# Product-key experts: the weight grid moves from TensorE one-hot matmuls to GpSimd scatter-add DMAs in DRAM

## The reference, cut to what matters

```python
s = einsum('thpc,hpnc->thpn', q, keys)         # 8 heads, 2 halves, 128 keys each
sv, si = top_k(s, 16)
cand = sv[:, :, 0, :, None] + sv[:, :, 1, None, :]
cv, ci = top_k(cand.reshape(T, 8, 256), 16)    # 16 experts a head and token
eid = e1 * 128 + e2
g = softmax(cv)
coef = g * gelu(x . u_tab[eid])
y = sum over heads and k of coef * v_tab[eid]  # residual added after
```

## Time and profile before

| | us |
|---|---|
| median of 3 runs | 3870.16 |
| lowest and highest | 3866.17, 3870.42 |
| profiled execution | 3867.6 |
| its span in the profile | 3865.9 |
| PE busy in the span | 3839.1 (99%) |
| DVE, ACT, POOL busy | 2532.3, 2065.4, 170.8 |
| granted clock of TensorE, mean | 0.997 |

### The profile page before, as it was taken

How to read it: one execution, slowest core, us unless ns; L and a number is a source line. 1 busy time by engine, 2 the same in 40 slices (tenths; PEclk the granted TensorE clock), 3 DMA queues, 4 the chain that set the end, 5 groups by cost and what they waited for, 6 DMA issues and landing times.

```text
span 3865.9 us, 58649 instructions
## 1 busy us (share of the span) xinstructions
PE 3839.1 (99%) x19628; PEld 3270.9 (85%) x19628; DVE 2532.3 (66%) x3843; ACT 2065.4 (53%) x3240; POOL 170.8 (4%) x150
## 2 busy tenths in 40 slices
PE   8999999999999999999999999999999999999999
PEld 8989988888888888888899889888888888888887
DVE  4565789878885555555564555889788875555555
ACT  5354444478885444444454544444688864444444
POOL 2110000000000000000121000000100000000000
PEclk9999999999999999999999999999999999999999
DMA  5455576655555666666454555666655556666665
GB/s 199 147 168 177 188 217 217 215 175 170 168 169 185 197 196 196 196 197 195 160 175 142 169 174 189 206 217 216 193 169 169 172 174 194 197 198 202 199 198 180
DMA packets 230743, 721.88 MB, mean 187 GB/s; under 512 B 29424, under 2 KB 58288, under 8 KB 230240
## 3 DMA queue, kind: packets, MB, share of 16 engines
q1 hardware_dynamic: 226640, 706.92, 57.0%
q0 software_dynamic: 3984, 13.37, 0.9%
HBM read 699.20 MB, written 6.29 MB: 182 GB/s over the span
## 4 chain that ended last, share of the span: by engine, by line
PE 96%; DVE 2%; DMA 1%; ACT 1%; issue 0%; DVEq 0%; SPq 0%; ACTq 0%
PE ps L2184 12%; PE ps L2185 12%; PE ps L2186 12%; PE ps L2108 12%; PE ps L2110 12%; PE ps L2109 12%; PE ps L1774 4%; PE ps L1775 4%; PE ps L1776 4%; PE ps L2161 2%; PE ps L1857 1%; PE ps L1859 1%; PE ps L1858 1%; PE ps L2122 1%; PE ps L2067 1%; DVE w_lo L1159 1%
## 5 line engine op out<-in xcount | busy, mean ns | idle before, releaser
L1159 DVE TENSOR_TENSOR w_lo<-w_raw,w_hi 128x1024 fp32r<-128x1024 f32 x1312 | 1633.4, 1246 | 1240.8 <-ACT w_hi L647 1210.1
L647 ACT ACTIVATE w_hi<-w_raw 128x1024 fp32r<-128x1024 f32 x1312 | 1389.8, 1061 | 1570.4 <-DMA w_raw<-in_v_tab 761.6
L2108 PE MATMUL ps<-w_hi,act_lo_t 128*128 128x512 f32 x2048 | 801.9, 392 | 1.1 <-DVE w_lo L1159 1.1
L2110 PE MATMUL ps<-w_hi,act_hi_t 128*128 128x512 f32 x2048 | 799.5, 390 | 0.0
L2184 PE MATMUL ps<-w_hi,act_lo_t 128*128 128x512 f32 x2048 | 797.9, 390 | 0.4 <-DVE w_lo L1159 0.3
L2186 PE MATMUL ps<-w_hi,act_hi_t 128*128 128x512 f32 x2048 | 796.9, 389 | 0.0
L2185 PE MATMUL ps<-w_lo,act_hi_t 128*128 128x512 f32 x2048 | 796.8, 389 | 0.0
L2109 PE MATMUL ps<-w_lo,act_hi_t 128*128 128x512 f32 x2048 | 796.6, 389 | 0.0
L2110 PEld LDWEIGHTS ps<-w_hi,act_hi_t 128*128 128x128 f32 x2048 | 384.2, 188 | 84.2
L2184 PEld LDWEIGHTS ps<-w_hi,act_lo_t 128*128 128x128 f32 x2048 | 384.4, 188 | 83.2 <-DVE w_lo L1159 1.9
L2186 PEld LDWEIGHTS ps<-w_hi,act_hi_t 128*128 128x128 f32 x2048 | 384.4, 188 | 80.0
(11 more groups left out here) (252 smaller groups left out, 2847.2 us busy)
## 6 DMA issues: line engine op xcount, KB each, us to landing
w_raw<-in_u SPq DMA_DIRECT2D x512, 512.0 KB, 3.5
w_raw<-in_v_tab SPq DMA_DIRECT2D x512, 512.0 KB, 3.7
w_raw<-in_dense SPq DMA_DIRECT2D x288, 512.0 KB, 3.5
big<-big SPq DMA_DIRECT2D x448, 32.0 KB, 3.0
x_spill<-big POOLq DMA_DIRECT2D x16, 256.0 KB, 4.6
big<-x_spill POOLq DMA_DIRECT2D x32, 128.0 KB, 4.0
big<-in_x_in SPq DMA_DIRECT2D x4, 512.0 KB, 5.1
big<-in_keys POOLq DMA_DIRECT2D x2, 1024.0 KB, 7.2
```

What stands on the lines that cost most here:

```text
L647: act.activation(w_hi[:, slot, :], w_raw[:, slot, :], ACT.Copy).then_inc(s_hi, 1)
L1159: dve.tensor_tensor(w_lo[:, slot, :], w_raw[:, slot, :], w_hi[:, slot, :].bitcast(F32), ALU.subtract).then_inc(s_lo, 1)
L2108: pe.matmul(o, act_lo_t[:, kb, t], w_hi[:, s % 4, c], start=kb == 0, stop=False)
L2110: ins = pe.matmul(o, act_hi_t[:, kb, t], w_hi[:, s % 4, c], start=False, stop=kb == KB - 1)
```

## The change

The grid is no longer built by TensorE. It lies in DRAM (`weight_grid`, 16384 x 256 floats, 16 MB). In the dense part of each layer SP writes zeros over it, 32 DMAs of 512 KB, one behind every four slab loads; in the first layer all dense slabs but the first four have one. DVE works out an element number for every pick (two more small steps in each top-k item). POOL then issues, for each of 16 items and each of 16 picks, one indirect DMA that adds 128 weights (one a token) into the grid: 256 a layer. Before an item it waits for the completion of the item of the head before in the same token block. POOL then reads the grid back in 32 chunks of 512 KB, beside table `v`, into two buffers `gb`, and DVE multiplies each chunk into `big` (`weigh`) just ahead of its use.

The softmax is cut in two batches of four heads: the first after turn 8, the second within turn 16. All turns but the last use the DVE transposes and the SP shuffles; only the last is still transposed by TensorE. The one before last lands in `last_quads`, which shares its memory with `cv` and `idx`, so its transpose waits for all scatter DMAs. The one-hot code on DVE, ACT and TensorE goes, and POOL's two fills of `big` with ones go.

```diff
+        grid = nc.dram_tensor("weight_grid", (N_KEYS * N_KEYS * T, 1), F32).ap()
+        idx = sb("idx", [P, ITEMS, TOPK], U32)
+        last_quads = nc.alloc_sbuf_tensor_at("last_quads", [P, TB, 512], F32, offset=stdv_base)
+        gb = sb("gb", [P, 2, CHUNK])
@@ SP
+                def fill(c):
+                    sp.dma_start(grid_chunk(c).rearrange("(p n) a -> p (n a)", p=P), gb[:, 0, :]).then_inc(s_filled, 16)
+                sp.wait_ge(s_zero, layer + 1)
+                with sp.Fori(1, U_TURNS) as i:
+                    dense_turn(i)                     # (i - 1 in the second layer)
+                    fill(i)
+                fill(0)
@@ POOL
-                pool.memset(at(K_TURNED + 2048, N_KEYS * T - K_TURNED - 2048), 1.0).then_inc(s_ones, 1)
-                pool.memset(at(K_TURNED, 2048), 1.0).then_inc(s_ones, 1)
+                pool.wait_ge(s_filled, 16 * U_TURNS * (layer + 1))
+                for n in range(ITEMS):
+                    h, tb = n // TB, n % TB
+                    if n % PER_BATCH == 0:
+                        pool.wait_ge(s_slots, BATCHES * layer + n // PER_BATCH + 1)
+                    if h:
+                        pool.wait_ge(s_scattered[tb], 16 * TOPK * (HEADS * layer + h))
+                    for k in range(TOPK):
+                        pool.indirect_dma_start(grid, bass.IndirectOffsetOnAxis(ap=idx[:, n, k:k + 1], axis=0),
+                                                cv[:, n, k:k + 1], None, compute_op=ALU.add).then_inc(s_scattered[tb], 16)
+                def weights(c):
+                    if c >= 2:
+                        pool.wait_ge(s_weighted, U_TURNS * layer + c - 1)
+                    pool.dma_start(gb[:, c % 2, :]..., grid_chunk(c)...).then_inc(s_gb[c % 2], 16)
@@ ACT
-                act.activation(cv[:, :, :], cv[:, :, :], ACT.Exp).then_inc(s_cexp, 1)
+                exponents(0)                          # ahead of turn 8
+                exponents(1)                          # ahead of turn 16
@@ DVE
+                yield lambda: tk_chain(dve.scalar_tensor_tensor(out=expert, in0=e12[:, 0, :], scalar=float(N_KEYS),
+                                                                in1=e12[:, 1, :], op0=ALU.mult, op1=ALU.add))
+                yield lambda: tk_chain(dve.tensor_scalar(di, expert, float(T), tcol[:, tb:tb + 1], ALU.mult, ALU.add))
+                def weigh(c, b):
+                    dve.wait_ge(s_shuffled[b], ...)
+                    dve.wait_ge(s_gb[b], ...)
+                    dve.tensor_tensor(rows, rows, gb[:, b, :]..., ALU.mult).then_inc(s_weighted, 1)
+                    if tb == 0 and isinstance(i, int) and i == SHUFFLED - 1:
+                        for half in range(TB):
+                            dve.wait_ge(s_scattered[half], 16 * TOPK * HEADS * (layer + 1))
+                quads_turn(U_TURNS - 2, 0, {4: lambda: weigh(0, 0)})
+                        if q % 4 == 2:                # in the blocks of table v
+                            weigh(i * 2 + (q // 4 + 1), 1 - q // 4)
@@ PE
-                        if scattering:
-                            scatter(i, s)
-                            slots(s)
-                            upright(before(i), s // 2)
```

More of the change, by code:

```diff
@@ L364, in expert_block, with grid_chunk, quads_of @@
             return whole_turn(i * 2 + q // 4)[:, q % 4]
+        def grid_chunk(c):
+            n = 4 * P * T
+            rows = grid[c * n:(c + 1) * n] if isinstance(c, int) else grid[bass.ds(c * n, n)]
+            return rows
+        def quads_of(j, b):
+            return last_quads if isinstance(j, int) and j == SHUFFLED - 1 else turned_t[:, b]
         def xs(tb, c):
@@ L412, in _ @@
                         load(s, s, dense[s], wait=False)
[L413 to L415 removed]
+                sp.wait_ge(s_zero, layer + 1)
+                with sp.Fori(1, U_TURNS) as i:
+                    if layer == 0:
+                        dense_turn(i)
+                    else:
+                        dense_turn(i - 1)
+                    fill(i)
+                fill(0)
+                if layer == 1:
+                    with sp.Fori(U_TURNS - 1, DENSE[layer] // RING) as i:
+                        dense_turn(i)
                 n0 = SLAB0["u", layer]
@@ L435, in u_turn @@
                         u_load(i, s)
[L436 to L441, removed]
+                        exchange(i, b, s, ends, begins)
                 u_turn(0, 0, False, 0)
@@ L626, in _ @@
                         pool.dma_start(at(F_GAIN + w * g, w), last_gain[:, w * g:w * (g + 1)]).then_inc(s_last_gain, 16)
+                done = 0
+                for c in range(U_TURNS):
+                    weights(c)
+                    while c >= 2 and done < BACK and 2 * KB + RING + 12 * done + 6 < 8 * (c - 2) + 4:
+                        back(done)
+                        done += 1
+                assert done == BACK, done
+                if layer == 0:
+                    pool.wait_ge(s_weighted, U_TURNS)
+                    pool.memset(gb[:, 0, :], 0.0).then_inc(s_zero, 1)
                 if layer == 0:
@@ L1023, in gelu @@
                     m = lin(i, 2, 2 * U_TURNS * layer + tb)
[L1024 to L1028, removed]
+                    if isinstance(i, int) and i == SHUFFLED and tb:
+                        act.wait_ge(s_upright, TB * layer + 1)
+                    elif not (isinstance(m, int) and m == 0):
+                        act.wait_ge(s_mix, m)
                     if shuffled:
```

397 lines of the change are left out of this document (151 added, 246 removed).

## The result

| | before, us | after, us |
|---|---|---|
| median | 3870.29 (4 runs, 3866.17 to 3874.0) | 4010.29 (4 runs, 4001.62 to 4017.71) |
| profiled execution, its span | 3867.6, 3865.9 | 4014.47, 4012.7 |
| ratio of after to before | | 1.036, 95% interval 1.034 to 1.039 |

A forecast was written before the change was run, and what follows sets the result against it. TensorE, busy for 99% of the span, was taken to bound the kernel. 3867.6 - 99.7 (TensorE work) + 8.4 (top-k turns) + 2 (fills, read-back) + 2 (POOL against DVE) gave 3780 us, range 3764 to 3885.

The forecast's parts named there:

- What leaves TensorE: Tables `u` of both layers: each stage falls to 697.8 us without grid and other transposes, 99.7 us saved.
- POOL's scatter: Beside table `u`: 256 indirect DMAs a layer at 1.34 us, 343 us in 480, done about turn 25, hidden.
- rival 2: Scatter too slow: above 1.87 us a DMA TensorE waits at turn 31; at 2.57, 4136 us. Chance 0.14.
- The shared port (rival 1): Top-k turns: POOL's indirect DMAs hold up every `lo` by 1.07 us, 103 in all, 3881. Chance 0.12.
- The top-k turns on DVE: Table `u`: two added steps make a turn 22.06 us against TensorE's 21.79, costing 8.4 us in all.
- The engines that carry it: DMA engines during the scatter: 31 ns a piece, 71 us an engine where 144 are free, hidden; limit 62 ns.
- The lowest price, 5 ns: DMA engines: lower price of a piece, from 16-byte runs, 2 x 2048 in 16 us taking 8.5%.
- Fills and read-back: Zero fills in dense parts and chunks read back beside table `v`, DMA share 0.61 to 0.69: costs 2 us.
- its own sign of being wrong: Slab loads: the prediction is wrong if `w_raw` lands later than 5.6 us for long.
- The clock: TensorE's clock stays at its upper level, 2.4 GHz, throughout; no change expected.
- The sum: Whole execution: 3867.6 - 99.7 + 8.4 + 2 = 3778.3, and 2 for POOL and DVE interfering: 3780 us.

The follow-up runs named there:

- three batches and quarters: The changed kernel with three softmax batches instead of two and each chunk read back in four DMAs of 128 KB: 3811.15 us, 0.986 of the kernel before.
- quarters: The changed kernel with each 512 KB read-back chunk split into four DMAs of 128 KB, one in two slabs: 3951.24 us, 1.022 of the kernel before.

## Why the prediction was wrong, point by point

**What leaves TensorE: right as a floor.** No run reached it: table `u` comes to 711.9 and 712.0 against 697.8 once the stall is gone, and to 709.1 at best.

**POOL's scatter: the step that failed.** "I take 1.34, since indices are work by the element: 343 us, done at about turn 25, hidden." That was the duration of a direct DMA of 2048 runs, between ends of 0.54 and 2.57. Measured: 1.54 alone, 0.30 between two issues (which the step had not counted at all), 0.37 more from `lo`, 2.21 together. The step's own limit was 1.87: undisturbed, 1.84, the scatter would just have fitted. With `lo` out of its way from turn 15 on it took 1.95 in the mean, and all but 7.9 us of the wait was gone. The bounds were right and the value in them was not: with no row of such an operation in the trace, and a limit only 1.4 times the value taken, the chance of 0.14 for rival 2 was too small. The mechanism of the loss was as that rival had it, place and all. It put the break-even at 2.05. The waits are 67.7 us in layer 0 and 63.4 in layer 1, 131 of the 234 us between the forecast and the profiled execution.

**Why not more than 68.** TensorE came to its wait at 1211.1 - 67.7 = 1143.4. DVE stood already, and POOL had 36 issues left from 1140.3 on. At the 2.27 us each of the 220 before they would have ended at 1222, and with the 3.5 us from there to TensorE's next matmul the wait would have been some 82. While DVE stood they took 1.84 each, which saved 15.

**The shared port (rival 1): right that the two contend, wrong on who pays.** `lo` did not grow (1.30 us at most). Something on DVE did: in the scatter's time the shift of 16 numbers took 0.46 us in place of 0.17 in a part of the turns. The line of it, 441 to 790 us, in after:

```profile
L1553 DVE TENSOR_SCALAR big<-big x14: 174/175/461, 478.3 to 769.7; 128x16 uint32<-128x16 uint32 x14
```

The same section of the Trainium skill counts such forms (`tensor_scalar`, a cast) among those that can take the port pair whole; the trace fits that, and no run here tested it.

**The top-k turns on DVE: right in kind, too small.** Taken: 22.06 us a turn and 8.4 in all. The timeline of DVE in after, `lo` at the start of two turns four apart, as the earlier trace rows:

```profile
663.95 1.23 DVE L1192 TENSOR_TENSOR w_lo<-w_raw,w_hi 128x1024 fp32r<-128x1024 f32 x1 [0.21 <-DVE cv L1573]
...
754.59 1.27 DVE L1192 TENSOR_TENSOR w_lo<-w_raw,w_hi 128x1024 fp32r<-128x1024 f32 x1 [0.21 <-DVE cv L1573]
```

That is 22.66 a turn. The added steps have 0.60 us from reduce to copy and not 0.42, since the second waits 0.16 for the first, and the shift and a cast add up to 0.36. Against 21.79 of TensorE it is 0.87 a turn, about 11 over 13 turns, less a lead of 1. The three turns from 507.45 to 574.63, ahead of the scatter, already took 22.39 in the mean, so at most 0.3 of the 0.6 over the forecast lies with POOL. The excess of the `u` stages over 697.8 in the run with three batches and quarters is 14.1 and 14.2; by this working some 20 of those 28 us are this term, which no run took away by itself. Taking the two steps out of each turn brought it to 22.04 (the mean of four turns from 681.56 to 769.73), but the stages gained only 2.8 and 1.6. The chain of that run names loads which landed after 4.9 and 4.5 us as the next thing (DMA share 0.90); how the rest is divided between them and DVE stays open.

**The engines that carry it: the size was off, the end right.** Taken 31 ns a piece, found 40 to 47, below the limit of 62. (The lowest price, 5 ns, misread its row: the earlier trace rows counts 128 packets and not 4096 runs, which is 1.36 us for 8 packets an engine, 170 ns each. Nothing in the sum used it.) In the stall, where little else runs, the row of the queue in after from 1140 to 1200 us is

```profile
q0 software_dynamic: 4617, 0.02, 22.7%
```

or 0.227 x 60 x 16 / 4617 = 47 ns. The DMA share rose to 0.91, and TensorE was not short of slabs for it. Of the rule in the Trainium skill, DMA: Bandwidth & Descriptors, "Specifications", that under 512 bytes an engine reads, modifies and writes, no run shows whether it happens here; they show only the price. A DMA which writes 128 single numbers takes 32 x 11 ns = 0.36 us of engine time, under 3 ns a number, and one which adds them 144 x 40 ns = 5.8 us, 45 ns a number.

**Fills and read-back: the second step that failed.** "I take 2 us." It was 69.3 beside table `v` (40.9 and 28.4) and 11.8 in the dense parts (8.4 and 3.4). The step had read right that a load of 512 KB by POOL once passed without harm. But it took that one case for all, and the loads now landed after up to 7.5 us, over the 5.6 that it had named as its own sign of being wrong. Why the one case did no harm isn't shown; beside table `v` ACT has the halves of the product to make between two `w_hi`, and the dense part has no such work. The 69.3 is also the largest figure on record: in five other kernels with the same read-back it is 42 to 50. The rise of the DMA share to 0.69, which I took to decide it, decided nothing: quarters have 0.68 and cost 2 to 3 us.

**The clock: a small miss.** I expected no change. In 1130 to 1206 us, where PE was busy for 13 of 76, the granted clock was 0.60 in the mean, and PE's first matmuls after the stall step 0.43 us, the 1.2 GHz level, until 1213.9. The six from 1211.13 to 1213.86 take 2.7 us in place of 1.4. In three batches and quarters, without the stall, no matmul of the two tables takes over 506 ns; in after some take up to 796.

**The sum, put right.** 3867.6 - 99.7 + 28.2 for the `u` stages outside of stalls + 8.9 in the dense parts + 5.7 beside table `v` = 3810.7, the profiled execution of three batches and quarters. After is that + 137.2 in `u` (131.1 the two stalls, 6 the clock behind them and short waits) + 2.9 in the dense parts + 63.6 for the 512 KB bursts = 4014.4. The change was worth 1.5% to the kernel before; it lost 5% by the turn at which the scatter starts and by reading back 512 KB at a time.

## What to carry to other kernels

Where a new kind of instruction must fit in a fixed time and no row shows its duration, compute the break-even first, and if it lies inside the bounds, give the overrun a chance of that size; count the gap behind each issue as well. A chain of many small GpSimd DMAs should start as early as its first data allow, since nothing tried here made its pace (2.2 us each) faster and kept its sums. And judge a transfer that shares the DMA engines with a tight ring of loads by what lands at once, not by the share of the engines that it takes.

## What was not expected of the hardware

- An indirect DMA of 128 numbers costs POOL 0.96 us if it writes and 1.54 if it adds, and 1.40 if it adds 64 numbers; 0.30 us lie behind each. (The first and the last from one execution each, 512 issues.)
- The same DMA is 32 pieces if it writes and 144 if it adds, 11 and 40 to 47 ns of an engine each.
- A `lo` (two SBUF operands) that is already running stretches an adding issue up to 2.6 us and isn't stretched itself (1.30 us at most); one that starts later hardly does (1.58 in the mean of 77). With one operand in PSUM it doesn't stretch it at all (1559 ns at most in 172).
- One 512 KB transfer issued by POOL made a load land after 7.5 us in place of 3.7; the same bytes in four of 128 KB, spread over eight slabs, left TensorE no wait in 1240 to 1860 us.
